# Feed-forward products as pairs of 64-row tiles on TensorE, with six split weight buffers

## The reference

```
def conv_ffn(u, w_up, conv_w, conv_b, w_down):
    hdn = causal_dwconv(u @ w_up, conv_w) + conv_b      # w_up: 1024 x 5632
    gate, val = jnp.split(hdn, 2, axis=-1)
    return (jax.nn.silu(gate) * val) @ w_down           # w_down: 2816 x 1024
...
    u = rms_norm(x, norm_gains[layer, 2])
    ff = conv_ffn(u, ffn_w_up[layer], ffn_conv_w[layer], ffn_conv_b[layer], ffn_w_down[layer])
    x = x + rms_norm(ff, norm_gains[layer, 3])
```

## Time and profile before

| | us |
|---|---|
| median of 3 runs | 950.01 |
| the runs | 950.29, 950.01, 949.82 |
| the profiled execution | 949.35 |
| its span | 947.7 |
| PE busy in it | 937.0 |
| loop of the first layer, from its second half of tile 3 on | 452.7 to 614.8 |
| loop of the second layer, likewise | 778.0 to 942.8 |

### The profile page before, as it was taken

How to read it: one execution, slowest core, us unless ns; L and a number is a source line. 1 busy time by engine, 2 the same in 40 slices (tenths; PEclk the granted TensorE clock), 3 DMA queues, 4 the chain that set the end, 5 groups by cost and what they waited for, 6 DMA issues and landing times.

```text
span 947.7 us, 17157 instructions
## 1 busy us (share of the span) xinstructions
PE 937.0 (99%) x6988; PEld 813.7 (86%) x6988; DVE 757.0 (80%) x1214; ACT 624.0 (66%) x1046; POOL 15.5 (2%) x28
## 2 busy tenths in 40 slices
PE   9999999999999999999999999999999999999997
PEld 7878789988889987889888888899888898888886
DVE  5787678555867998787998888877976779988886
ACT  7566767347766775577676666777556777666665
POOL 0000000000000000000000000003000000000000
PEclk9999999999999999999999999999999999999999
DMA  8735454743253534364566656655545646766562
GB/s 303 259 114 149 141 165 144 229 141 123 89 179 113 154 119 130 90 180 133 180 219 199 188 183 188 214 162 156 158 127 165 201 119 180 226 185 184 196 193 96
DMA packets 44654, 158.07 MB, mean 167 GB/s; under 512 B 4896, under 2 KB 6432, under 8 KB 44576
## 3 DMA queue, kind: packets, MB, share of 16 engines
q1 hardware_dynamic: 43568, 154.29, 52.3%
q0 software_dynamic: 576, 2.10, 0.7%
q10 hardware_dynamic: 432, 0.59, 0.3%
HBM read 155.91 MB, written 1.05 MB: 166 GB/s over the span
## 4 chain that ended last, share of the span: by engine, by line
PE 90%; ACT 4%; DVE 4%; DMA 0%; issue 0%; ACTq 0%; DVEq 0%
PE psum L431 88%; PE psum L440 2%; DVE w_lo L409 1%; ACT w_hi L396 1%; DMA raw<-in_pieces 0%; ACT scr L3156 0%; ACT normed L572 0%; DVE scr L3166 0%; DVE scr L3474 0%; ACT u_both L2978 0%; DVE scr L3148 0%; DVE scr L3142 0%; ACT L3266 0%; DVE feat L3468 0%; ACT scr L3451 0%
## 5 line engine op out<-in xcount | busy, mean ns | idle before, releaser
L409 DVE TENSOR_TENSOR w_lo<-raw,w_hi 128x1024 fp32r<-128x1024 f32 x281 | 338.4, 1218 | 43.3 <-ACT w_hi L396 42.7
L396 ACT ACTIVATE w_hi<-raw 128x1024 fp32r<-128x1024 f32 x281 | 290.2, 1051 | 42.4 <-PE psum L431 32.7
L431 PE MATMUL psum<-u_both,w_hi 128*128 128x512 f32 (+1 forms) x704 | 162.8, 381 | 1.3 <-ACT w_hi L396 1.3
L431 PEld LDWEIGHTS psum<-u_both,w_hi 128*128 128x128 f32 x704 | 127.4, 188 | 28.0 <-ACT w_hi L396 3.8
L431 PE MATMUL psum<-w_hi,u_hi 128*128 128x512 f32 x336 | 135.5, 404 | 0.5 <-ACT w_hi L782 0.3
L431 PE MATMUL psum<-w_hi,u_lo 128*128 128x512 f32 x336 | 130.9, 391 | 0.0
L431 PE MATMUL psum<-w_lo,u_hi 128*128 128x512 f32 x336 | 103.8, 390 | 0.0
L431 PEld LDWEIGHTS psum<-u_both,w_lo 128*128 128x128 f32 x672 | 86.1, 191 | 3.3
L431 PE MATMUL psum<-u_both,w_lo 128*128 128x256 f32 x672 | 87.5, 283 | 0.0
L431 PE MATMUL psum<-u_hi,w_hi 128*128 128x256 f32 x320 | 81.7, 288 | 0.0
L431 PE MATMUL psum<-u_lo,w_hi 128*128 128x256 f32 x320 | 80.0, 283 | 0.0
(11 more groups left out here) (334 smaller groups left out, 1415.9 us busy)
## 6 DMA issues: line engine op xcount, KB each, us to landing
raw<-in_pieces SPq DMA_DIRECT2D x287, 512.0 KB, 3.7
post_gain<-in_norm_gains POOLq DMA_DIRECT2D x4, 512.0 KB, 4.1
x_res<-in_x SPq DMA_DIRECT2D x4, 256.0 KB, 5.5
const<-in_table SPq DMA_DIRECT2D x1, 928.0 KB, 6.3
out_x<-x_res SPq DMA_DIRECT2D x1, 512.0 KB, 2.6
cols<-in_cols SPq DMA_DIRECT2D x1, 384.0 KB, 6.2
raw<-in_pieces ACTq DMA_DIRECT2D x1, 256.0 KB, 4.7
raw<-in_pieces SPq DMA_DIRECT2D x1, 256.0 KB, 4.4
```

Source lines behind the costliest of these rows:

```text
L396: act.q.activation(w_hi[slot[i]][:, :], raw[i % RAW][:, :], ACT.Copy).then_inc(act.done, act.mark("hi", i))
L409: dve.q.tensor_tensor(w_lo[slot[i]][:, :], raw[i % RAW][:, :], w_hi[slot[i]][:, :].bitcast(F32), ALU.subtract).then_inc(dve.done, dve.mark ...
L431: return pe.q.matmul(o, lhs, rhs, start=start, stop=stop, **kw)
```

## The change

`pe_tile_rows` takes the place of `pe_up` and `pe_down` in iterations 5 to 21 of both layers (tiles 0 to 4, the down product of tile 17 and the ends stay as they were). Each 128-row matmul becomes two matmuls of 64 rows, with as many columns: one on rows 0 to 63 and one on rows 64 to 127. `row_pair` issues them alternately on two different outputs (gate and value; token half 0 and 1), so that the two row tiles write different banks. A second pass does the other 64 rows of each, with the banks crossed. The order in an iteration is: up high, first pass; down, first pass; up high and low, second pass; down, second pass; up low, first-pass rows. Where a bank goes from one row tile to the other, PE waits for its own earlier pass (marks `"rows"` and `"down"`). All six split buffers are lent to the loop, and the oldest is taken. `split_by` is raised by one piece at tile 4 and by two from tile 5 on.

```
--- before.py
+++ after.py
@@ -235,11 +235,13 @@
 
 def piece_slots(n):
 
-    slots, ring = [], 0
+    slots, last = [], [-1] * (SPLIT + 2)
     for i in range(n):
         early = [i - at for at in (*FFN_AT, C_AT) if 0 <= i - at < 2]
-        slots.append(SPLIT + early[0] if early else ring % SPLIT)
-        ring += not early
+        lent = FFN_AT[0] <= i < C_AT - LAST_DOWN or FFN_AT[1] <= i < n - LAST_DOWN
+        best = SPLIT + early[0] if early else min(range(SPLIT + 2 if lent else SPLIT), key=lambda k: last[k])
+        slots.append(best)
+        last[best] = i
     return slots
 
 
@@ -429,6 +431,14 @@
     def mm(o, lhs, rhs, start=True, stop=True, loose=False):
         kw = {"skip_group_check": True} if loose else {}
         return pe.q.matmul(o, lhs, rhs, start=start, stop=stop, **kw)
+
+    def row_pair(first, products):
+
+
+        for one, other in products:
+            for g, (o, lhs, rhs, start, stop) in ((first, one), (64 - first, other)):
+                last = pe.q.matmul(o, lhs[g:g + 64], rhs[g:g + 64], start=start, stop=stop, skip_group_check=True)
+        return last
 
     def mm3(o, lhs, rhs, start, stop):
         (lh, ll), (rh, rl) = lhs, rhs
@@ -3071,6 +3081,55 @@
                 last = mm(psum[:, 2 * (j % 2) + i, 0:S], lo[:, i, kk, :], u_f[0][:, k, :], False, k == KT - 1, True)
         return last
 
+    def pe_tile_rows(l, j):
+
+        ups = [pe_take()[0] for _ in range(2)]
+        pe.wait_ge(dve, "up_read", l, j - 2)
+        d = j - FFN_LAG
+
+        def up(part, first, high, start=False, stop=False):
+            hi = view((w_hi if high else w_lo)[slot[ups[part]]], 0, 2, KT // 2, P)
+
+            def one(i, kk):
+                k, o = part * KT // 2 + kk, psum[:, 2 * (j % 2) + i, :]
+                turn = u_both[:, k, :, :].rearrange("p a s -> p (a s)") if high else u_f[0][:, k, :]
+                return o if high else o[:, 0:S], hi[:, i, kk, :], turn, start and kk == 0, stop and kk == KT // 2 - 1
+
+            return row_pair(first, [[one(i, kk) for i in range(2)] for kk in range(KT // 2)])
+
+        def down(n, part, first, weights, start=False):
+            def one(t, c):
+                return (psum[:, 4 + 2 * t + c, :], hid[d % HIDDEN][part][:, t * P:(t + 1) * P],
+                        weights[slot[n]][:, c * NC:(c + 1) * NC], start, False)
+
+            return row_pair(first, [[one(t, c) for t in range(ST)] for c in range(2)])
+
+        up(0, 0, True, start=True)
+        up(1, 0, True).then_inc(pe.done, pe.mark("rows", l, j, 0))
+        n, _ = pe_take()
+        pe.wait_ge(dve, "hid", l, d)
+        if d:
+            pe.wait_ge(pe, "down", l, d - 1)
+        down(n, 0, 0, w_hi, start=d == 0)
+        down(n, 1, 0, w_hi)
+        pe_lo(n)
+        down(n, 0, 0, w_lo).then_inc(pe.done, pe.mark("rows", l, j, 1))
+        pe.wait_ge(pe, "rows", l, j, 0)
+        for part in range(2):
+            up(part, 64, True)
+        for part in range(2):
+            last = up(part, 64, False)
+        last.then_inc(pe.done, pe.mark("rows", l, j, 2))
+        pe.wait_ge(pe, "rows", l, j, 1)
+        down(n, 0, 64, w_hi)
+        down(n, 1, 64, w_hi)
+        down(n, 0, 64, w_lo).then_inc(pe.done, pe.mark("used", n))
+        pe.also("down", l, d)
+        pe.wait_ge(pe, "rows", l, j, 2)
+        for part in range(2):
+            up(part, 0, False, stop=part == 1).then_inc(pe.done, pe.mark("used", ups[part]))
+        pe.also("up", l, j)
+
     def pe_up(l, j):
 
         pieces = [pe_take()[0]]
@@ -3252,15 +3311,18 @@
     def pe_ffn(l):
         pe_ups_first(l)
         for j in range(2, FT + FFN_LAG - LAST_DOWN):
-            if j < FT:
+            if FFN_LAG <= j < FT:
+                pe_tile_rows(l, j)
+            elif j < FT:
                 pe_up(l, j)
-            if j >= FFN_LAG:
+            else:
+                pe.wait_ge(pe, "down", l, j - FFN_LAG - 1)
                 pe_down(l, j - FFN_LAG)
         pe_down_ends(l)
 
     def split_by(l, j):
 
-        return FFN_AT[l] + 4 + 2 * j + max(0, j - FFN_LAG)
+        return FFN_AT[l] + 4 + 2 * j + max(0, j - FFN_LAG) + min(2, max(0, j - FFN_LAG + 2))
 
     def act_ffn(l):
         act.q.preload_act_table_set("silu_and_others")
```

## The result

The changed kernel takes 958.88 us (median of 4 runs, 958.37 to 960.39) where the kernel before took 949.91 on the same chip (949.31 to 950.29): ratio 1.010, 95% interval 1.0087 to 1.0113. It is slower by 9.0 us where 941 was forecast; the time is that of rival 1 (958). The profiled execution took 958.37 with a span of 956.7.

What follows compares the result with a forecast made beforehand. PE was taken as the bound, busy 937.0 of 947.7 us. Against the profiled 949.35: entries +4.0, steady tiles -16.0, exits +3.0, height changes +0.8, so 941; own range 936 to 947, 8 in 10 range 936 to 961.

Steps and rivals of the forecast that it cites:

- rival 1: Feed-forward tiles: the 13 ns stay whatever the height, only new waits count, +8.6, so 958 us; chance 0.33.
- Does the 13 ns shrink?: Feed-forward matmuls: on 64 rows spacings fall to 0.216 and 0.109 us, a tile takes 7.79 us, 0.50 less.
- Do two row tiles run side by side?: Row-tile pairs: loads and matmuls of different row tiles overlap; the doubled number of instructions costs nothing by its count.
- Rival 3: Row-tile pairs: full-width loads or full-rate streams don't overlap, 2.3 us a tile, +78, about 1035 us; chance 0.10.
- The waits of PE for itself: Crossed passes: each waits for the earlier pass on its banks; at least 1.3 us of cover, so zero.
- Changing the tile height: Four places where PE goes between 128 and 64 rows: about 0.2 us each, 0.8 in all.
- Entry: Tile 5 of each layer: PE waits for split pieces, +2.0 us a layer, +2.4 at the old spacing.
- Steady tiles: 16 tiles a layer: 0.50 us won in each, -16.0 us; DVE and ACT tight but in time.
- rival 4: Steady tiles: DVE becomes the bound at 7.7 to 8.0 us a tile, 941 to 948 us; within the forecast's 0.52.
- Exit: Tile 21: PE waits for `hid_lo`, 1.8 us in the first layer and 1.2 in the second, together +3.0.

Runs made afterwards that it cites:

- rows_10_to_20: The changed kernel with its new order for tiles 10 to 20 only, the other tiles computed as before: 951.71 us, ratio 1.0014 to 1.0033.
- six_buffers_only: The changed kernel's six split buffers and earlier splits, with no tile in the new order: 951.56 us, ratio 1.0024.
- full_height_same_order: The changed kernel's order, banks, waits and splits, but each pair is one matmul on 128 rows: 961.51 us, ratio 1.0128.
- rows_splits_early: The changed kernel with the second pieces of up tiles 3, 4 and 5 split one place earlier: 961.47 us, ratio 1.0126.
- one_row_tile_alone: The changed kernel with only the first matmul of each pair kept: 1093.53 us.
- rows_to_tile_20: The changed kernel with its new order for tiles 5 to 20, tile 21 done in the order of before: 957.06 us, ratio 1.0066 to 1.0094.
- bf16_row_tiles: The changed kernel with its high products in bf16, up operands at a 4-byte step, down operands packed: 956.27 us.

## Why the prediction was wrong

The step that failed is "Does the 13 ns shrink?". I took the 64-row plain-float rows as the nearest, because of their tile shape and the way of issuing. They were neither fp32r nor compared at equal width, and the earlier trace rows, 64 weight columns on 128 rows at 3 ns more, already said that the difference from the earlier trace rows did not belong to height. I named that as rival 1's evidence and gave it 0.33. And the rows themselves were a choice. Over the whole span of before, the groups by shape have the same 64-row passes as long as fp32r's 389 and 283, and passes of full height nearly as short as the 269 of the earlier trace rows:

```profile
L431 PE MATMUL psum<-feat 64*64 64x256 f32 x144 | 11.8, 389 | 0.0
L431 PE MATMUL psum<-feat 64*64 64x128 f32 x144 | 7.8, 280 | 0.0
L431 PE MATMUL psum<-scr,feat 128*128 128x128 f32 x32 | 4.0, 274 | 0.0
```

So a short record was no sign of a low height. What counted was the step from one moving word to the next, and the only rows with fp32r said 0.226. In place of a gain of 16.0 us the steady tiles lost 0.6; the rest of the sum was that of rival 1. (The range's lower end has a slip that changed nothing: its own terms, 32 x 0.6 won, half of 7.0 lost and 0.8, give 934.5 and not 936.)

- **Do two row tiles run side by side?** Right. The second starts 3 to 4 ns later, and a pair takes what one full-height matmul took. Rival 3 (1035) is out.
- **The waits of PE for itself.** Right inside the tiles, up to 0.02 us a tile (8.307 against 8.287): the first five matmuls of 512 columns behind a run of 256-column ones start 228 to 236 ns apart, and the new order has such a place twice a tile. This is 0.7 us in all, and the full-height kernel has it too. Where down products follow one another (rows_10_to_20, six_buffers_only) the lone one of the exit loses 0.33 us to its wait; in after other products lie between, and it loses nothing. There I had not looked.
- **Changing the tile height.** 0.2 us a change was right: in rows_10_to_20 each of the four costs 0.20. But in after 0.8 was too much. At the two entries the change lies in the stall. At the exits it takes 0.2 us, and the wait for `w_early` behind it is 0.21 us where full_height_same_order, without a change, waits 0.40; so it adds nothing there either.
- **Entry.** Right, by the numbers of rival 1: 2.4 us a layer forecast, 2.3 and 2.4 measured, with waits of 1.88 on `w_hi` (1.9 said) and 0.19 on the low part (0.6 said). rows_splits_early shows that it is not the place of the up pieces alone: the wait moves to the down piece and keeps its size.
- **Steady tiles.** DVE (7.04 us) and ACT never hold PE; at 8.31 us they had room to spare, so that rival 4 was not put to the test.
- **Exit.** The chain was right. The waits in the record are 1.31 + 0.21 where 1.8 was said and 0.75 + 0.21 where 1.2 was, but each costs more from start to start: with the change of height the exits lose 2.2 and 1.6 us.

Together 4.7 at the entries, 0.6 in the steady tiles and 3.8 at the exits: 9.1, which is all of the +4.8 and +4.3. That rival 1's +8.6 came so near is partly luck: its 0.8 for the heights added nothing net, and its 3.0 for the exits was as much too small.

Open is why the same stall of 1.9 us lowers the clock behind it in both layers of full_height_same_order and one_row_tile_alone, in the first alone in rows_to_tile_20, in the second alone in bf16_row_tiles, and in neither in after, and what exactly PE waits for in the mixer's gap.

## What to carry to other kernels

Before tiles are reshaped to save a fixed excess per matmul, find which operand it belongs to: here a row of the same type on other shapes was missing, and rows of another type, taken from one short window, misled; the same groups over the whole span would have warned. In a loop in which PE is 99% busy, an order that asks for inputs earlier is a debt paid once at each end, and moving one producer's work ahead only moved the stall on. Two more buffers together with earlier splits took the 0.65 us waits of the old order away for good; for the stall of the new order that isn't shown. And when two kernels with the same work differ by microseconds far from the edit, look in the densest stretch of small instructions for a gap that the profile calls issue: a few instructions more or less ahead of it may be the whole difference.

## What the runs showed of the hardware that was not expected

- The excess of a 512-column fp32r or bf16 matmul over its columns at full clock is 13 ns with a moving operand at a 4-byte step, 2.7 ns packed (a tile of ones), and none at the 1.2 GHz level (0.426 and 0.214 us apart, above); the stationary operand's step and the rows don't matter, and half of its columns win nothing.
- A change between 128-row and 64-row products costs 0.20 us where no wait hides it (rows_10_to_20, 209 + 337 ns from start to start for 120 + 227), and a second row tile starts 3 to 4 ns behind the first.
- Lone 64-row matmuls back to back, with PE busy 120.00 of 120.00 us, ran at a granted clock of 0.50 once it had fallen; pairs of them ran at 1.00. The Trainium skill (TensorE: Matmul & The Clock Gate, section What's actually happening) has the clock follow how busy PE has been recently; here PE was busy by the record all the time, on half of the rows, and the clock stayed at the lower level.
- In a stretch of small matmuls PE can stand for 0.9 to 3.5 us with nothing that the profile shows to wait for. The Trainium skill (Runtime: NRT & Kernel Launch, section Instruction fetch mechanics) says that crossing a 16 KB block is mostly hidden. In most places it is; in the mixer of six kernels here it was not, as far as the gaps are that fetch, and it was worth up to 6.0 us with the half clock that followed.
